# Additions of squares for the two normalisations of h: from VectorE to GpSimd

## What is computed

```python
def rmsnorm(x, g):
    xf = x.astype(jnp.float32)
    y = xf * lax.rsqrt(jnp.mean(xf * xf, -1, keepdims=True) + EPS)
    return (y * g.astype(jnp.float32)).astype(x.dtype)

def layer(x, ...):
    h = rmsnorm(x, g_pre_mix)
    p = jnp.einsum('bld,dc->blc', h, w_in)
    ...
    x = x + rmsnorm(m, g_post_mix)
    h = rmsnorm(x, g_pre_ffn)
    f = jax.nn.silu(h @ w_gate) * (h @ w_up)
    x = x + rmsnorm(f @ w_down, g_post_ffn)
```

## Time and profile before

| what | value |
|---|---|
| time, median of 3 runs | 1376.72 us (1376.61 to 1376.72) |
| profiled execution | 1376.75 us, its span 1375.2 us |
| busy: TensorE, VectorE, ScalarE, GpSimd | 1331.9, 713.2, 455.9, 36.3 us |
| mean granted TensorE clock | 0.987 of full speed |
| chain that ended last, by engine | TensorE 86%, VectorE 7%, ScalarE 3% |

### The profile page before, as it was taken

How to read it: one execution, slowest core, us unless ns; L and a number is a source line. 1 busy time by engine, 2 the same in 40 slices (tenths; PEclk the granted TensorE clock), 3 DMA queues, 4 the chain that set the end, 5 groups by cost and what they waited for, 6 DMA issues and landing times.

```text
span 1375.2 us, 25654 instructions
## 1 busy us (share of the span) xinstructions
PE 1331.9 (97%) x10681; PEld 1298.9 (94%) x10681; DVE 713.2 (52%) x887; ACT 455.9 (33%) x638; POOL 36.3 (3%) x60
## 2 busy tenths in 40 slices
PE   6999999999999999999889999999999999999997
PEld 6999988989999999999889999898999999999996
DVE  6846677495444434222377456856844453441225
ACT  4532224453222222322254511344422222222222
POOL 3000002000000000000020000010000000000000
PEclk9999999999999999999989999999999999999999
DMA  6322113222222222221342221231222223222221
GB/s 221 93 78 80 61 62 97 77 77 77 92 89 79 92 92 78 96 88 58 113 132 78 77 79 47 67 108 62 84 85 92 88 80 92 91 77 92 86 85 65
DMA packets 110473, 119.09 MB, mean 87 GB/s; under 512 B 4576, under 2 KB 107128, under 8 KB 110136
## 3 DMA queue, kind: packets, MB, share of 16 engines
q1 hardware_dynamic: 107456, 108.57, 24.9%
q0 software_dynamic: 2496, 8.27, 2.1%
q10 hardware_dynamic: 440, 1.09, 0.2%
HBM read 113.23 MB, written 4.69 MB: 86 GB/s over the span
## 4 chain that ended last, share of the span: by engine, by line
PE 86%; DVE 7%; ACT 3%; issue 2%; DMA 1%; ACTq 0%; DVEq 0%; SPq 0%
PE ps L491 27%; PE ps L493 27%; PE ps L492 26%; DVE x L1185 1%; ACT h_hi L923 1%; DVE r_post L1169 1%; PE ps L663 1%; PE ps L521 1%; DVE y L1180 1%; PE ps L641 1%; PE ps L667 1%; DVE w_lo L1149 1%; ACT w_hi L904 1%; DVE r_pre L1222 1%; PE ps L731 1%
## 5 line engine op out<-in xcount | busy, mean ns | idle before, releaser
L491 PE MATMUL ps<-h_hi,w_hi 128*128 128x272 f32 x2240 | 660.1, 295 | 25.4 <-ACT h_hi L923 12.0
L493 PE MATMUL ps<-h_lo,w_hi 128*128 128x272 f32 x2240 | 649.3, 290 | 0.0
L492 PE MATMUL ps<-h_hi,w_lo 128*128 128x272 f32 x2240 | 646.7, 289 | 0.0
L491 PEld LDWEIGHTS ps<-h_hi,w_hi 128*128 128x128 f32 x2240 | 424.9, 190 | 38.2 <-ACT h_hi L923 22.8
L492 PEld LDWEIGHTS ps<-h_hi,w_lo 128*128 128x128 f32 x2240 | 427.1, 191 | 1.8 <-issue 1.4
L493 PEld LDWEIGHTS ps<-h_lo,w_hi 128*128 128x128 f32 x2240 | 424.1, 189 | 0.0
L1149 DVE TENSOR_TENSOR w_lo<-w_raw,w_hi 128x1024 fp32r<-128x1024 f32 (+1 forms) x208 | 244.8, 1181 | 271.7 <-ACT w_hi L904 269.8
L904 ACT ACTIVATE w_hi<-w_raw 128x1024 fp32r<-128x1024 f32 (+1 forms) x208 | 211.7, 1021 | 230.7 <-DMA w_raw<-in_w_down 146.0
L491 PE MATMUL ps<-f_hi,w_hi 128*128 128x272 f32 x704 | 204.1, 290 | 0.0
L493 PE MATMUL ps<-f_lo,w_hi 128*128 128x272 f32 x704 | 203.1, 288 | 0.0
L492 PE MATMUL ps<-f_hi,w_lo 128*128 128x272 f32 x704 | 202.4, 287 | 0.0
(11 more groups left out here) (177 smaller groups left out, 1085.7 us busy)
## 6 DMA issues: line engine op xcount, KB each, us to landing
w_raw<-in_w_in SPq DMA_DIRECT2D x52, 512.0 KB, 3.6
w_raw<-in_w_gate SPq DMA_DIRECT2D x44, 512.0 KB, 3.6
w_raw<-in_w_up SPq DMA_DIRECT2D x44, 512.0 KB, 3.6
w_raw<-in_w_down SPq DMA_DIRECT2D x36, 512.0 KB, 3.4
w_raw<-in_w_out SPq DMA_DIRECT2D x16, 512.0 KB, 3.4
w_raw<-in_w_down SPq DMA_DIRECT2D x16, 256.0 KB, 2.7
tab<-in_table POOLq DMA_DIRECT2D x2, 1536.0 KB, 7.1
st_s<-in_state_ret POOLq DMA_DIRECT2D x8, 256.0 KB, 5.3
```

What stands on the lines that cost most here:

```text
L491: pe.matmul(out, wh, hi[:, cols(half)], start=begins, stop=False)
L492: pe.matmul(out, wl, hi[:, cols(half)], start=False, stop=False)
L493: mm = pe.matmul(out, wh, lo[:, cols(half)], start=False, stop=ends)
```

## The change

`add_squares` moves from VectorE's block to GpSimd's, with the same operands, waits and signals. On GpSimd it is called for both halves of norm 0 at the start of a layer, ahead of the wait for `mix_free`, and for both halves of norm 1 after the stores, ahead of the wait for their end. VectorE gets a wait for the last addition of the second half ahead of the reciprocal of `r_pre`, in both norms, since the copies out of PSUM that follow write into the buffers that hold squares.

```diff
@@ block of GpSimd, start of a layer
+                def add_squares(norm, half):
+
+                    for pair in range(1, 4):
+                        n = 6 * norm + 3 * half + pair
+                        pool.wait_ge(pre_sq.sem, pre_sq.at(l, 8 * norm + 4 * half + pair + 1))
+                        if pair > 1:
+                            pool.wait_ge(pre_acc.sem, pre_acc.at(l, n - 1))
+                        pool.tensor_tensor(acc[:, :, cols(half)], acc[:, :, cols(half)],
+                                          square_room(half, pair), ALU.add).then_inc(pre_acc.sem, 1)
+
+                add_squares(0, 0)
+                add_squares(0, 1)
                 pool.wait_ge(mix_free, l + 1)
...
+                add_squares(1, 0)
+                add_squares(1, 1)
                 pool.wait_ge(stored.sem, stored.at(l + 1, 0))
@@ block of VectorE
-                def add_squares(norm, half):
...
                 def then_low(pair):
-                    if pair == 1:
-                        add_squares(0, 0)
                     low_tiles(0, G_PRE_MIX, 1, pair)
                 update(l, 1, then_low)
-                add_squares(0, 1)
...
                     if u in (2, 3):
+                        if u == 2:
+                            after(pre_acc, 6)
                         recip_pre(0, u - 2)
...
                         split(l, FFN0 + 3)
-                    add_squares(1, half)
...
                     if first:
+                        after(pre_acc, 12)
                         recip_pre(1, 0)
```

## The result

The changed kernel takes **1404.87 us** (median of 5 runs, 1403.42 to 1406.24), the kernel before 1376.72 beside it: a ratio of 1.0202, 95% interval 1.0191 to 1.0214. The change costs 28.1 us. The direction was forecast, the size was not: 11.5 us were, and 1404.87 lies above the range.

The account below looks back on a forecast made before the run. The prediction took TensorE, busy 97%, to bound the kernel. Its terms gave 9p - 3.97 per layer, 5.75 us at p = 1.08, +11.5 for two layers on 1376.75: 1388.3 us; range over all cases 1372.8 to 1392.5.

Parts of the forecast that it names:

- What bounds the kernel: Whole kernel: TensorE, busy 97%; VectorE's time counts only where TensorE waits for it, in each layer's two normalisations of h.
- What is taken from VectorE: Both normalisations: VectorE loses its additions of squares, saving 2.24 us in the first and 0.92 us in the second, per layer.
- rival B: Both normalisations: GpSimd's additions do not interfere with VectorE; 1.9 us gained per layer, 3.8 together, 1373.0 us; chance 0.22.
- The addition's length and what it holds: Both normalisations: a GpSimd addition lasts 0.72 to 1.44 us, taken as 1.08, and holds VectorE for all of it.
- p: Duration of one GpSimd addition of 544 elements, taken as 1.08 us between 0.72 and 1.44.
- rival C: Both normalisations: exclusion, but VectorE goes first and additions wait for its idle time or reciprocals; 1375.8 us; chance 0.25.
- Norm 0 with turns: First normalisation of h in each layer: additions and VectorE alternate, delaying root and TensorE by 5p - 3.05, +2.35 us.
- The marks that the forecast set: Signs of turns: VectorE rows last 1.2 to 2 us; ACT's last square, first normalisation, ends near 40.4 instead of 38.1.
- 3p - 0.81: First normalisation, first half: three additions push VectorE by 3p, less 0.81 us that it stood idle anyway.
- Norm 1 with turns: Second normalisation of h in each layer: additions and VectorE alternate, delaying TensorE by 4p - 0.92, +3.40 us.
- What moves behind GpSimd's additions: After the first normalisation's additions: memset of z_p and 13 table loads come later, landing at 55.4, needed at 55.9; cost nothing.
- Rival D: Setup matmuls, each layer: table loads need over 13.8 us and TensorE waits; at 15.5 us, 1391.7 us; chance 0.05.

Follow-up runs that it names:

- The writer kernel: Changed kernel with the table loads issued before the first normalisation's additions and each GpSimd addition replaced by a same-size memset: 1372.97 us, ratio 0.9968.
- the kernel with the fillers: Changed kernel with small matmuls of unread result put near TensorE's stops, ahead of unit 4 and in the second normalisation's first half: 1403.9 us, ratio 1.0190.
- the one with norm 1 alone: Changed kernel with only the second normalisation's additions on GpSimd, the first's kept on VectorE: 1387.73 us, ratio 1.0074.

## Why the forecast was right in direction and wrong in size

*What bounds the kernel.* Right. TensorE's stops in the two normalisations are the places where the additions cost something, and outside them and the stretch of the late loads the delay hardly grows: 0.9 us in the mixers of layer 1, -0.2 behind the last norm 1.

*What is taken from VectorE.* Right. The writer kernel gives it alone: 3.5 us in the four normalisations, where the working of rival B had 3.8. That the whole time, 1373.0, met B's figure to the tenth is luck: it takes in 1.5 us from layer 1's mixers in the profiled execution.

*The addition's length and what it holds.* Right in mechanism and close in size. p was taken at 1.08 between 0.72 and 1.44; an addition takes 1.33 us and holds VectorE 1.07 to 1.17. That the middle fits is in part luck. It was taken between the two ends for want of a row, and it stood for the addition's duration; with 1.33 the sum would have been 1392.8. The sum needs what VectorE loses, and that this is less than the duration was not forecast. In proportion the Trainium skill's figures (GPSIMD Engine Reference, section 3.1) had given an estimate of 1.19 for the duration; the trace has 1.33. That GpSimd gets its turn after the running operation, against rival C, shows in the first row of its timeline: 1.85 us, of which some 0.5 are waiting.

*Norm 0 with turns.* 2.35 us were forecast in each layer and 2.69 and 3.45 measured. The marks that the forecast set are there: ACT's last square ends at 40.12 + 0.64 = 40.76 (forecast near 40.4), and the reciprocal of r_post starts at 27.23, 2.60 later than before, where 3p - 0.81 is 2.43. The path was not quite the one forecast. The sum let the shift reach TensorE through the root; the root does come 2.7 us later, but TensorE's stop for it stays at 0.38 us, because it has already lost 2.5 us at three h_lo tiles. Stops for h_lo were forecast for norm 1 alone.

*Norm 1 with turns.* The waits were right: TensorE's waits for VectorE there grow from 3.9 us in the kernel before to 7.4 in layer 0 and to 8.1 in layer 1, by 3.5 and 4.2, against 3.40. What the sum lacks is the clock: 1.7 us in each layer on top, which together give 5.2 and 5.9 of the measured 5.3 and 6.0. The forecast named this as something that would add to it, in its last sentence, and priced it at nothing.

*What moves behind GpSimd's additions.* **This is the step that failed.** The forecast followed the tables to the one matmul that needs them, found half a microsecond of slack, and put the move at nothing. It cost 10.7 us by the changed kernel's own delays (4.2 + 0.4 in layer 0, 6.1 in layer 1), and the late loads alone, without the change, cost 11.7. Two things were missing. The forecast's 13.3 us from first issue to last landing were never measured: they use the median of 5.3 us for the last load. In the kernel before the 13 loads of layer 0 take 15.0 us (14.97 to 30.0) and those of layer 1 13.2; in the changed kernel they take 16.3 and 16.5. With 15.0 the forecast's own sum gives 57.1, past the 55.9 at which TensorE needs the tables. Above all, the forecast looked only at the transfer that moved and not at those that it would then run beside: the weight loads of units 5 to 7 go from 3.5 to 4.8 us up to 9 to 13, and the first of them has the second root of norm 0 queued behind its copy on ScalarE. Rival D, the late tables, got 0.05 and a price of 2 x 1.7 us on top; it had the right transfers, and a victim that shows only when the root goes first; the one that stood in front, the weights of unit 5, it did not have.

| term, both layers, us | forecast | measured | missed by |
|---|---|---|---|
| norm 0, additions | 4.7 | 6.1 | 1.4 |
| loads behind the additions | 0 | 10.7 | 10.7 |
| mixers of layer 1, cause open | 0 | 0.9 | 0.9 |
| norm 1, waits for VectorE | 6.8 | 7.7 | 0.9 |
| norm 1, clock | 0 | 3.4 | 3.4 |
| sum | 11.5 | 28.8 | 17.3 |

The sum of the measured terms is 28.8 against 28.9 us between the two spans; since all but the two rows of norm 1 are cut out of TensorE's delay, this checks those two alone, 11.1 against 11.3. Three fifths of the error are the loads, a fifth the clock in norm 1; of the loads' 10.7 us, some 2.5 are half clock as well. What stays open: why layer 1 costs more than layer 0 in each of the parts (3.45 to 2.69, 6.1 to 4.2, 6.0 to 5.3). In norm 0, 0.6 us of it arise ahead of the additions, and at the set-up the weight load of unit 5 takes 11.2 us instead of 9.1; no run was made to tell why.

## What to carry to other kernels

When work is put at the head of an engine's queue, follow what it pushes back beyond its own consumer: which transfers of other queues fall into the same microseconds, and which engine has something urgent queued behind one of them. An engine that is idle in the profile need not be free to read: here an operation of 1.3 us on GpSimd took 1.1 us from VectorE, more than the 0.72 that it saved. And where a stall is forecast for TensorE, the stretch behind it belongs in the sum: here the clock fell to half in four places where it had not before.

## What was not expected of the hardware

- Table loads of 2.9 MB issued by GpSimd from 42.3 us on stretched three weight loads of 512 KB on SyncE's queue from 3.5 to 4.8 us up to 9.1, 12.3 and 10.8. In the kernel before, the tables are issued from 14.97 on and have landed at 30.0; the weight loads of units 2 and 3 overlap them, with 6.5 and 7.2 us, and the next is issued at 35.48. The same two take 6.3 and 7.0 us in the changed kernel, with no table under way, so there the tables cost the weights next to nothing.
- A GpSimd copy of 544 elements took 0.64 us and held a VectorE operation for 0.44; an addition of the same size took 1.33 and held it for 1.1; a memset took 0.55 and held nothing.
- The clock did not go by the length of the last stop alone: in the kernel with the fillers it fell behind a stop of 1.20 us at unit 6 of layer 0, and stayed at 1.00 behind a stop of the same 1.20 us in unit 4 of layer 1. Around one stop of 2.7 us in the mixers of layer 1 it was 0.88 over 28 us in the changed kernel and 1.00 in the one with norm 1 alone.
